# The low half of a weight panel in four POOL instructions of 512 columns

## What is computed

```python
x = first_block(x, ...)    # one layer
return second_block(x, ...)    # two layers
```

## Time and profile before

| | |
|---|---|
| median of 3 runs | 2927.16 us (2926.36 to 2931.26) |
| profiled run | 2926.75 us, span 2924.9 us |
| granted TensorE clock, mean | 0.958 |
| busy PE, DVE, ACT, POOL | 2707.8, 1280.1, 998.6, 939.4 us |
| largest POOL group | L884, 206 instructions |
| its idle time | 1959.4 us, all of it ended by ACT's cast L900 |
| DMA read from HBM | 217 MB, 75 GB/s over the span |

### The profile page before, as it was taken

The page is one execution under the profiler, slowest core; times in us unless marked ns, Lnnn a source line. Parts: engine busy times, 40 slices in busy tenths (PEclk is TensorE's granted clock), DMA queues, the critical chain, the costliest instruction groups (busy, mean ns, idle before and its releaser), DMA issues.

```text
span 2924.9 us, 29646 instructions
## 1 busy us (share of the span) xinstructions
PE 2707.8 (93%) x12430; PEld 2179.7 (75%) x12430; DVE 1280.1 (44%) x2067; ACT 998.6 (34%) x1152; POOL 939.4 (32%) x210
## 2 busy tenths in 40 slices
PE   5999999999999879797999999999988799999999
PEld 4787767787888667675677888888767567788887
DVE  5243465356523646668624311133666862431111
ACT  3423433243322445333324321234532432332121
POOL 2333331433444322112124343443211213434442
PEclk9899999999999989998999999999999899999999
DMA  4222212222332211111022223322111102223322
GB/s 136 65 72 72 73 58 65 92 88 87 101 101 85 89 58 44 44 58 44 29 72 86 95 93 101 101 87 87 44 44 44 58 29 72 87 87 100 101 94 79
DMA packets 206704, 221.01 MB, mean 76 GB/s; under 512 B 3713, under 2 KB 197467, under 8 KB 206443
## 3 DMA queue, kind: packets, MB, share of 16 engines
q1 hardware_dynamic: 206064, 218.97, 23.4%
q10 hardware_dynamic: 507, 0.15, 0.0%
HBM read 217.01 MB, written 2.10 MB: 75 GB/s over the span
## 4 chain that ended last, share of the span: by engine, by line
PE 76%; DVE 14%; ACT 6%; issue 1%; POOL 1%; DMA 1%; DVEq 0%; SPq 0%; ACTq 0%
PE psum L438 66%; ACT wh L900 2%; PE psum L563 2%; PE psum L661 2%; PE psum L670 2%; DVE tmp L1638 1%; POOL wl L884 1%; DVE ul L1388 1%; DVE score L1809 1%; PE psum L686 1%; DVE top L1807 1%; DVE dec L1492 1%; DVE stat L1634 1%; DVE normed L1449 1%; DVE sqsum L1400 1%
## 5 line engine op out<-in xcount | busy, mean ns | idle before, releaser
L884 POOL TENSOR_TENSOR wl<-raw,wh 128x2048 fp32r<-128x2048 f32 (+1 forms) x206 | 939.2, 4565 | 1959.4 <-ACT wh L900 1959.4
L438 PE MATMUL psum<-uh,wh 128*128 128x512 f32 x2024 | 817.5, 404 | 32.4 <-issue 17.0
L438 PE MATMUL psum<-ul,wh 128*128 128x512 f32 x2024 | 802.2, 396 | 0.0
L438 PE MATMUL psum<-uh,wl 128*128 128x512 f32 x2024 | 801.2, 396 | 0.0
L900 ACT CAST wh<-raw 128x2048 fp32r<-128x2048 f32 (+1 forms) x206 | 387.0, 1879 | 313.4 <-DMA raw<-in_w_ffn_out 118.8
L438 PEld LDWEIGHTS psum<-uh,wh 128*128 128x128 f32 x2024 | 389.5, 192 | 135.2 <-issue 37.5
L438 PEld LDWEIGHTS psum<-uh,wl 128*128 128x128 f32 x2024 | 388.4, 192 | 83.6
L438 PEld LDWEIGHTS psum<-ul,wh 128*128 128x128 f32 x2024 | 389.5, 192 | 79.9 <-issue 1.9
L438 PE MATMUL psum<-fh,wh 128*128 128x512 f32 x528 | 205.4, 389 | 0.0
L438 PE MATMUL psum<-fl,wh 128*128 128x512 f32 x528 | 205.4, 389 | 0.0
L438 PE MATMUL psum<-fh,wl 128*128 128x512 f32 x528 | 205.4, 389 | 0.0
(11 more groups left out here) (310 smaller groups left out, 3570.2 us busy)
## 6 DMA issues: line engine op xcount, KB each, us to landing
raw<-in_w_in SPq DMA_DIRECT2D x78, 1024.0 KB, 5.2
raw<-in_w_ffn_in SPq DMA_DIRECT2D x44, 1024.0 KB, 5.1
raw<-in_w_up SPq DMA_DIRECT2D x22, 1024.0 KB, 5.1
raw<-in_w_ffn_out SPq DMA_DIRECT2D x16, 1024.0 KB, 5.1
raw<-in_w_down SPq DMA_DIRECT2D x8, 1024.0 KB, 5.0
raw<-in_w_out SPq DMA_DIRECT2D x8, 1024.0 KB, 5.1
raw<-in_w_ffn_out SPq DMA_DIRECT2D x8, 768.0 KB, 4.4
raw<-in_w_o SPq DMA_DIRECT2D x4, 1024.0 KB, 5.0
```

The lines of the kernel that those rows point to most:

```text
L438: ins = mm(dst, x, y, start=first and i == 0, stop=last and i == len(todo) - 1)
L884: nc.gpsimd.tensor_tensor(wl[p % 3][:, w], raw[p % 3][:, w], wh[p % 3][:, w].bitcast(F32), ALU.subtract).then_inc(S.lo_done, 1)
```

## The change

POOL's loop makes the low half of a panel in pieces of 512 columns: four instructions for a panel of 2048 columns, three for one of 1536. Only the first stands behind the wait for ACT's cast, and only the last raises `lo_done`. What is computed, the buffers, the semaphores' counts and every other engine's code are the same.

```diff
+LOW_PIECE = 512
...
         def _(pool):
             for p in range(n_panels):
                 nk, width = panels[p][1:3]
-                w = slice(0, nk * width)
                 pool.wait_ge(S.hi_done, p + 1)
-                nc.gpsimd.tensor_tensor(wl[p % 3][:, w], raw[p % 3][:, w], wh[p % 3][:, w].bitcast(F32),
-                                        ALU.subtract).then_inc(S.lo_done, 1)
+                for c0 in range(0, nk * width, LOW_PIECE):
+                    w = slice(c0, c0 + LOW_PIECE)
+                    ins = nc.gpsimd.tensor_tensor(wl[p % 3][:, w], raw[p % 3][:, w], wh[p % 3][:, w].bitcast(F32), ALU.subtract)
+                ins.then_inc(S.lo_done, 1)
```

## The result

The changed kernel takes **2858.78 us** (median of four runs, 2853.03 to 2864.07) where the kernel before takes 2926.8 beside it: a ratio of 0.9764, 95% interval 0.9737 to 0.979. That is 68 us less. Two of the four runs take 2853 to 2854 us and two near 2864, for a reason that stayed open. The profiled one is of the first two, so the two profiled spans, 2924.9 and 2851.2 us, differ by 73.7 us.

A forecast was written before the change was run, and what follows sets the result against it. PE's matmuls (busy 93%) were taken to bound the kernel; only the chain's DVE part, some 410 us, could move. Shorter DVE holds summed to 47.3 us, taking 2926.75 to 2879.5 us, range 2852 to 2921.

The forecast's parts named there:

- DVE gets in between two pieces: Held DVE instructions take turns with POOL's pieces, waiting at most 1.25 us instead of up to 4.6.
- (b): Rival, 9%: DVE doesn't get in between pieces and is held through all four; slower, 2940 us.
- Top-k: Sparse attention's top-k, L1812, two places: the held instruction ends 3.3 us earlier each, 6.7 us gained (6 to 7).
- Softmax: Softmax scaling, L1638 and L1634: eight places gain 17.6 us (11 to 26), three with shorter PE waits 2 (0 to 4).
- Low half of the merged branches: L1671 before each output projection, three times: PE goes on earlier, 2.8 us each, 8.4 us gained.
- Gather and scaling: Gather before the second block's norm, L1400: 5 us gained (2 to 6.6); scaling behind it, L1388: 1 (0 to 1.5).
- Decay copies: Chunk cores, L1480 and L1538, eight copies ending 3.3 us earlier: 0.7 us kept each, 5.6 gained (1.6 to 18).
- Start: First panels, where PE waits for POOL: later panels and a quicker first gather, net 0 (3 lost to 1.4 gained).
- Feed-forward: Feed-forward stages, no PE gap, 2.7 us of slack: eleven panels of the first at risk, 1 us lost (0 to 5).
- (a): Rival, 13%: DVE wins its turns but the next thing is late anyway; 6 to 22 us gained, about 2912.
- (c): Rival, 6%: nothing measurable; holds shrink but both effects cancel, 2927 within 6 us.
- (d): Rival, 2%: POOL starved by DVE work in the feed-forward stages, PE waits there, and the gain is gone.

The follow-up runs named there:

- 2814: Kernel with a piece length per stage (512, 256 or 128 columns) plus a semaphore wait before each next piece of a panel: 2814.06 us, ratio 0.9615.
- the silent POOL: Against the changed kernel, POOL subtracts only 64 columns of each panel and PE reads the high part for the low: 2762.45 us, ratio 0.9438.

## Why the prediction was right, and where it was not

The forecast was 2879.5 us with a range of 2852 to 2921, and faster at 82%. The time lies in the range, near its lower end: the mechanism was right, the sum of 47.3 us too small by 21 against the medians and by 26 against the profiled span. The sum counted PE's waits, and PE's idle time did fall by 49.6 us. The missing part is the 24.1 us that PE is less busy with the same matmuls, for which the sum had no term. That the waits agree so well is in part luck: the cores gave less than forecast, the gather and the attention more.

- **A piece takes 1.25 us.** The median is 1.29. POOL's time a panel is 5.1 us in the top-k row and up to 6.1 where DVE takes turns.
- **DVE gets in between two pieces.** Right at 512 columns without exception, and so (b) fell. The Trainium skill, GPSIMD Engine Reference, section "Instruction dispatch", on which (b) leaned, says that consecutive instructions are no barrier between POOL's cores. The traces are in keeping with it in part: records overlap by 42 ns, and with pieces of 256 and 128 some turns are missed, until a wait parts the pieces. That the cores' overlap is what makes DVE miss a turn isn't shown. The Trainium skill, SBUF — State Buffer, section "Who interferes with whom", calls the ports that DVE and GpSimd share an exclusive lock for the whole of one instruction; the trace agrees (and 2927, 2885, 2859, 2838 us by length).
- **Top-k** 6.7: measured 2 x 3.3 in PE's waits.
- **Softmax** 19.6: PE's waits for the line fell by 19.9. The views by line gave the right ceiling and the right part of it.
- **Low half of the merged branches** 8.4: the two late merges, which hold little else, measure 5.3 and 5.4, not 2.8. By the starts of the matmuls, 4.89 us lay between two at the gap of before and 1.84 lie there now: 3.05 us, as forecast (though what PE waits for now is another L1675, and not L1690). **The term that was mis-sized is the clock**: the ten matmuls behind the old gap start 0.43 us apart and not 0.23, 2.0 us, and the first of them takes 0.34 more than usual; that is 2.3 together, and at 1.45 us of waiting only 0.1 of it is left. 3.05 + 2.2 = 5.3. At the first projection the old gap ends the stretch of the windowed attention, so the clock's part stands in the next stretch, for which nothing was forecast: PE is busy for 3.3 us less there, some 2.2 of them behind this gap. The rest comes from the norm, where 3.91 us lay between two matmuls and 2.65 lie there now.
- **The same term over the whole kernel** is 81 slow matmuls fewer; at 0.2 us each that is an estimate of 16 us, of the 24.1 that PE is less busy and of the missing 26. This is an account, not shown by an experiment of its own: no kernel holds the gaps and changes the clock. The kernel without PE's waits for POOL has 36 slow matmuls fewer, is busy for 3.2 us less and shows no gain that can be measured, so the term isn't simply added in every place.
- **Gather and scaling** 6: measured 8.2.
- **Decay copies** 5.6 at 0.7 each, and 2 for the rotation of the keys in the same stretches: the three cores gained 4.1, and two of them nothing. The rotation's two holds fell from 4.19 and 4.11 us to 2.32 and 2.14. The turns are strict there. Timeline of after, in the first core of the second block:

```profile
1104.35 5.37 POOL L888 TENSOR_TENSOR wl<-raw,wh 128x512 fp32r<-128x512 f32 x4 [21.42 <-ACT wh L904]
1105.40 0.26 DVE L1484 COPY small<-dec 128x2 f32<-128x2 f32 x1 [4.30 <-ACT dec L1024]
...
1106.20 0.97 DVE L1488 TENSOR_TENSOR dec<-dec,gk 128x256 f32<-128x256 f32 x1
1107.10 1.51 DVE L1490 TENSOR_TENSOR dec<-dec,gq 128x256 f32<-128x256 f32 x1
1108.53 1.35 DVE L1496 TENSOR_TENSOR dec<-dec,gq 128x128 f32<-128x128 f32 x1
1109.80 0.28 DVE L1496 TENSOR_TENSOR dec<-dec,gk 128x128 f32<-128x128 f32 x1
```

  The copy is quick, and then three instructions are held for a piece each; when POOL is done, DVE is 0.4 us ahead of before. I had put the value between rows 5 and rows 6; it is at rows 5.
- **Start** 0: measured 4.0 gained, and all of it is busy time (-4.1); PE's idle time is the same, so in waits the 0 was right. PE's waits for POOL there have grown, as forecast, from 1.93 and 4.62 us to 3.70 and 5.45. That such waits weigh nothing is shown for the kernel before alone.
- **Feed-forward** -1: the slack is there and thin, as the sum said. Timeline of after, against the earlier trace rows:

```profile
732.60 6.03 POOL L888 TENSOR_TENSOR wl<-raw,wh 128x512 fp32r<-128x512 f32 x4 [5.84 <-ACT wh L904]
...
733.99 2.24 DVE L1752 TENSOR_TENSOR tmp<-tmp 128x1024 f32<-128x1024 f32 x1
```

  POOL takes 6.03 us and not 4.61: 1.42 more, of the 2.7 that were left. Only one multiply gets in, not the subtract, and PE loses nothing.
- **(a), the gain given back**: the opposite; PE had no other wait close behind. **(c)** and **(d)** fell too.

## What to carry to other kernels

If DVE works from SBUF beside long POOL instructions, the length of one POOL instruction is what each held DVE instruction pays, so cut POOL's work into pieces, shorter where DVE comes in rows and PE waits for it, longer where PE needs POOL's result soon; with pieces below 512 columns a wait between them was worth 12.6 us here. Read how much there is to gain by silencing POOL once (165 us here) and not from the list of visible holds alone (47 by my sum). A forecast made of waits leaves out what the shorter gaps do to PE's clock: when a gap of PE shrinks, add the matmuls behind it that no longer run at the lower clock: 2.2 us for a gap of 4.5 that became 1.5.

## What the runs showed of the hardware

- POOL's two-input subtraction has a small fixed part: medians of 0.26 us for 32 columns, 0.46 for 128, 0.74 for 256, 1.29 for 512, 2.40 for 1024.
- POOL instructions that follow without a wait overlap by 42 ns in their records; DVE took its turn at all such borders with pieces of 512 and more, and missed it in two to four cases a run with 256 and 128, each time through two to thirteen pieces. A wait on a semaphore costs 0.12 us a piece (from 42 ns of overlap to 78 ns of gap), and with it no turn was missed.
- What the last 52 us are, between 2814 and the 2762 of the silent POOL, is not settled; the cores (21.5 us), the start (14.5) and the windowed attention (7.4) are the largest stretches of it.
- DVE instructions with an operand in PSUM, and MAX8, MATCH_REPLACE8, RECIPROCAL and TENSOR_REDUCE, never take over 0.03 us more than their shortest when they begin beside POOL, in the traces of before and after; the second L1671 in the earlier trace rows, with both inputs in SBUF, took 5.57 us and not 1.23.
